# A hybrid decoder trunk on one core: block transposes and small tiles in a triangular inverse, and another order of entries, FFN ends, head and tail

## The reference

```python
for l in range(DEPTH):                                   # DEPTH = 2, D_FF = 2816
    h = rms_norm(x, ffn1_norm[l]); x = x + 0.5 * swiglu(h, w_gate, w_up, w_down)
    proj = rms_norm(x, mix_norm[l]) @ w_in[l]            # 1024 -> 3080
    aq, ak, av, pu, dq, dk, dv, dz, db, da = split(proj) # 3x256, 256, 4x512, 4, 4
    ya = dilated_attention(rope(aq), rope(ak), av)       # 4 heads of 64, 3 patterns
    yb = multiscale_pool(pu, pool_w[l], pool_scale[l])   # windows 2, 4, 8, 16
    yc = gated_deltanet(dq, dk, dv, dz, db, da, ...)     # 4 heads of 128, chunks of 64
    x = x + concat(ya, yb, yc) @ w_out[l]
    h = rms_norm(x, ffn2_norm[l]); x = x + 0.5 * swiglu(h, w_gate2, w_up2, w_down2)
return rms_norm(x, final_norm)
# in gated_deltanet, per head and chunk of 64 tokens (decay: a lower triangle):
A = strict_lower((k * beta) @ k.T) * decay
T = triangular_solve(eye + A, eye)                       # the inverse
u, w = T @ (v * beta), T @ (k * beta * exp(g))
```

## Time and profile before

| | before |
|---|---|
| median of 3 runs | 1093.78 us |
| profiled execution | 1093.62 us |
| its span in the trace | 1091.8 us |
| mean granted clock of PE | 0.997 of full speed |
| busy: PE, PE weight load, DVE, ACT, POOL | 97%, 84%, 67%, 56%, 21% |

### The profile page before, as it was taken

The page is one execution under the profiler, slowest core; times in us unless marked ns, Lnnn a source line. Parts: engine busy times, 40 slices in busy tenths (PEclk is TensorE's granted clock), DMA queues, the critical chain, the costliest instruction groups (busy, mean ns, idle before and its releaser), DMA issues.

```text
span 1091.8 us, 18536 instructions
## 1 busy us (share of the span) xinstructions
PE 1060.0 (97%) x6251; PEld 922.2 (84%) x6251; DVE 736.9 (67%) x1153; ACT 616.0 (56%) x1077; POOL 231.7 (21%) x257
## 2 busy tenths in 40 slices
PE   7999999899999999999999999999999999999997
PEld 6888888798987788888878888888988878888885
DVE  5666666878745766666676666668785657666665
ACT  6555555847644655555665555566665546555554
POOL 2212111295300121121122121112003003211212
PEclk9999999999999999999999999999999999999998
DMA  9766666562312476666646666666532035766660
GB/s 296 238 194 190 191 183 181 139 194 78 135 40 72 141 216 188 192 191 190 183 133 208 194 191 190 183 185 167 162 115 79 2 116 163 207 189 193 190 193 38
DMA packets 251895, 178.23 MB, mean 163 GB/s; under 512 B 5875, under 2 KB 237576, under 8 KB 251720
## 3 DMA queue, kind: packets, MB, share of 16 engines
q1 hardware_dynamic: 250880, 175.66, 54.3%
q0 software_dynamic: 336, 1.71, 0.4%
q10 hardware_dynamic: 632, 0.23, 0.1%
HBM read 176.53 MB, written 1.05 MB: 163 GB/s over the span
## 4 chain that ended last, share of the span: by engine, by line
PE 83%; DVE 10%; ACT 5%; issue 1%; DMA 0%; ACTq 0%; DVEq 0%
PE bank L678 28%; PE bank L681 15%; PE bank L660 11%; PE bank L661 10%; PE bank L662 10%; DVE Wl L1647 4%; PE bank L1015 2%; ACT Wh L1219 1%; DVE X L1692 1%; PE bank L991 1%; DVE xr L1823 1%; PE bank L723 1%; ACT X L1277 1%; DVE VT L1834 1%; DVE early L1865 1%
## 5 line engine op out<-in xcount | busy, mean ns | idle before, releaser
L1647 DVE TENSOR_TENSOR Wl<-raw,Wh 128x1024 fp32r<-128x1024 f32 x330 | 424.6, 1296 | 102.3 <-ACT Wh L1219 102.2
L1219 ACT ACTIVATE Wh<-raw 128x1024 fp32r<-128x1024 f32 x330 | 337.1, 1053 | 78.2 <-PE bank L662 75.6
L678 PE MATMUL bank<-X,Wh 128*128 128x512 f32 x1344 | 334.7, 391 | 0.0
L678 PEld LDWEIGHTS bank<-X,Wh 128*128 128x128 f32 x1344 | 246.7, 188 | 47.6
L577 POOL TENSOR_TENSOR gact<-gact,pooled 128x256 f32<-128x256 f32 x88 | 79.2, 900 | 626.4 <-DVE gact L1743 462.2
L681 PEld LDWEIGHTS bank<-X,Wl 128*128 128x128 f32 x1344 | 183.0, 190 | 14.0 <-DVE Wl L1647 1.2
L681 PE MATMUL bank<-X,Wl 128*128 128x256 f32 x1344 | 187.8, 283 | 0.0
L660 PE MATMUL bank<-Wh,aH 128*128 128x512 f32 x352 | 139.0, 395 | 2.0 <-DVE aL L1764 1.6
L661 PE MATMUL bank<-Wl,aH 128*128 128x512 f32 x352 | 138.0, 392 | 0.0
L662 PE MATMUL bank<-Wh,aL 128*128 128x512 f32 x352 | 137.1, 389 | 0.0
L1316 ACT ACTIVATE dec<-bank 128x256 f32<-128x256 f32 x88 | 33.6, 382 | 123.2 <-PE bank L681 122.2
(11 more groups left out here) (244 smaller groups left out, 1302.0 us busy)
## 6 DMA issues: line engine op xcount, KB each, us to landing
raw<-in_ffn_w_gate SPq DMA_DIRECT2D x88, 512.0 KB, 4.0
raw<-in_ffn_w_up SPq DMA_DIRECT2D x88, 512.0 KB, 3.7
raw<-in_ffn_w_down SPq DMA_DIRECT2D x88, 512.0 KB, 4.4
raw<-in_w_in SPq DMA_DIRECT2D x50, 512.0 KB, 3.9
raw<-in_w_out SPq DMA_DIRECT2D x16, 512.0 KB, 4.0
cst<-in_consts POOLq DMA_DIRECT2D x1, 1536.0 KB, 7.0
xr<-in_x SPq DMA_DIRECT2D x2, 512.0 KB, 4.4
norm_w<-in_final_norm SPq DMA_DIRECT2D x1, 512.0 KB, 5.7
```

The lines of the kernel that those rows point to most:

```text
L678: nc.tensor.matmul(b[:, :], piece(Wh, s)[:, k, :], X[:, k, :, :], start=k == 0, stop=False)
L1219: return nc.scalar.activation(Wh[:, s, :], raw[:, s, :], ACT.Copy).then_inc(hi_cast.sem, 1)
L1647: return nc.vector.tensor_tensor(Wl[:, s, :], raw[:, s, :], Wh[:, s, :].bitcast(F32), ALU.subtract).then_inc(lo_cast.sem, 1)
```

## The change

1. **Inverse.** LEVELS is (2, 4, 8, 16). There P is made of the even blocks' columns alone (64 of 128). The transposes on PE (8 for the start, 8 per level) and ACT's copies of them are gone: DVE makes DT from D, and the first D from dt0, by transposes of 32x32 blocks (128x512 in one instruction). Level 32 is `quarter_p` and `quarter_d` with tiles of 32x32, level 64 is `half_p` and `half_d` with tiles of 64x64. The casts of output pieces 29 and 30 leave the levels: Wh goes behind the last copies of the inverse, Wl behind `out_norm(1)`.
2. **Entry of the mixer.** `att_part` 6 and 7 move into the inverse (`att_late`, behind `quarter_p` and `half_p`) and use the scaled x. `row_root` stands behind j = 2. On DVE the splits 4 to 7 and the Wl of pieces 2 and 3 stand before the roots, the xs operations are cut in two around a Wl, and small copies (prm) come later. The entry of FFN2 and the next layer's FFN1 have the splits 4 to 7 earlier too, and FFN2's first two Wl among the updates of xr.
3. **End of an FFN.** `hid`, aH and aL of the last tile are made in two halves of 128 tokens; PE waits for each, and for aL only before the third product.
4. **Head and tail.** The norm weights' transfers move from ACT's queue to POOL's. In the tail DVE makes quarter (0,0) in one operation and scales (1,1), ACT scales (0,1) and (1,0), POOL weighs the last three quarters; four stores, three from SP and one from ACT.

```diff
-POS_GATES, POS_QK, POS_V, POS_Z, FIRST_OUT = 8, 9, 17, 21, 25
+POS_GATES, POS_QK, POS_V, POS_Z, POS_LATE, FIRST_OUT = 6, 7, 15, 19, 23, 25
-LEVELS = (2, 4, 8, 16, 32, 64)
+LEVELS = (2, 4, 8, 16)
...
+            for n, weight in enumerate((ffn1_norm, mix_norm, ffn2_norm)):
+                pool.dma_start(nrm_rows[n * DEPTH * KT:(n + 1) * DEPTH * KT, :],
+                              weight.rearrange("l (k c) -> (l k) c", c=P)).then_inc(norms_in.sem, 16)
...
+                    high, low_part, i = (half_ah, half_al, f + 1) if c == 0 else (ah_done, al_done, (f + 1) * TILES)
+                    pe.wait_ge(*high.at(layer, i))
+                    nc.tensor.matmul(acc[c][n][:, :], aH[:, 1, t], Wh[:, 5, q], start=False, stop=False)
+                    nc.tensor.matmul(acc[c][n][:, :], aH[:, 1, t], Wl[:, 5, q], start=False, stop=False)
+                    pe.wait_ge(*low_part.at(layer, i))
+                    return nc.tensor.matmul(acc[c][n][:, :], aL[:, 1, t], Wh[:, 5, q], start=False, stop=True)
...
+                            m = nc.tensor.matmul(bank[4 + c][odd, h * 32:(h + 1) * 32], LT[even, u, odd], Dm[even, u, even],
+                                                 start=True, stop=True)
...
+                        nc.tensor.matmul(bank[6 + c][q[1], at], DT[q[1], u, q[1]], PM[q[1], u, 0:32], start=True, stop=True)
+                        nc.tensor.matmul(bank[6 + c][q[0], at], PM[q[1], u, 0:32], DT[q[1], u, q[1]], start=True, stop=True)
+                        m = nc.tensor.matmul(bank[6 + c][q[2], at], PM[q[3], u, 0:32], DT[q[3], u, q[3]],
+                                             start=True, stop=True)
...
                 for n in range(len(LEVELS)):
                     for c in range(HALVES):
                         level_p(n, c)
-                    if n:
-                        for c in range(HALVES):
-                            turn_d(n - 1, c)
-                    if n == len(LEVELS) - 1:
-                        turn_qk()
                     for c in range(HALVES):
                         level_d(n, c)
+                for c in range(HALVES):
+                    quarter_p(c)
+                att_late(6)
+                for c in range(HALVES):
+                    quarter_d(c)
+                turn_qk()
+                for c in range(HALVES):
+                    half_p(c)
+                att_late(7)
+                for c in range(HALVES):
+                    half_d(c)
...
                 follow(3)
-                hidden_high(layer, f, TILES - 1, 1)
+                act.wait_ge(*half_mul.at(layer, f + 1))
+                act.wait_ge(*downs_done.at(layer, (f + 1) * TILES - 2))
+                nc.scalar.activation(aH[:, 1, 0:P], hid[:, 1, 0:P], ACT.Copy).then_inc(half_ah.sem, 1)
+                act.wait_ge(*mul_done.at(layer, (f + 1) * TILES))
+                nc.scalar.activation(aH[:, 1, P:], hid[:, 1, P:], ACT.Copy).then_inc(ah_done.sem, 1)
...
+                def turn_blocks(n, c):
+                    u = slice(4 * c, 4 * c + 4)
+                    dve.wait_ge(*d_done.at(layer, 2 * (n - 1) + c + 1))
+                    nc.vector.transpose(DT[:, u, :].rearrange("p u d -> p (u d)"),
+                                        Dm[:, u, :].rearrange("p u d -> p (u d)")).then_inc(dt_done.sem, 1)
...
                 out_norm(1)
+                lo_mix(layer, 29)
+                lo_mix(layer, 30)
                 dve.wait_ge(*att_hi.at(layer, 1))
```

More of the change, by code:

```diff
@@ L512, in weigh_final @@
                 pool.wait_ge(norm_w_in.sem, 16)
-                for i in range(3):
+                for i in range(1, 4):
                     c, b = divmod(i, 2)
@@ new lines, in half_p, with half_d @@
+                def half_p(c):
+                    pe.wait_ge(*d_done.at(layer, 8 + c + 1))
+                    for h, u in units(c):
+                        m = nc.tensor.matmul(bank[4 + c][EVEN:, h * EVEN:(h + 1) * EVEN], LT[0:EVEN, u, EVEN:],
+                                             Dm[0:EVEN, u, 0:EVEN], start=True, stop=True)
+                    m.then_inc(p_done.sem, 1)
+                def half_d(c):
+                    pe.wait_ge(*pm_done.at(layer, 10 + c + 1))
+                    pe.wait_ge(*dt_edge.at(layer, c + 1))
+                    for h, u in units(c):
+                        m = nc.tensor.matmul(bank[6 + c][0:EVEN, h * EVEN:(h + 1) * EVEN], PM[EVEN:, u, 0:EVEN],
+                                             DT[EVEN:, u, EVEN:], start=True, stop=True)
@@ L1298, in enter @@
                     square(1, 1)
-                    for c in range(HALVES):
-                        inverse(layer, n, c)
                 act.wait_ge(*turned.at(layer, 4 * n + 4))
@@ L1303, in enter @@
                     split(j)
-                if first:
-                    for c in range(HALVES):
-                        inverse(layer, n, c)
+                for c in range(HALVES):
+                    inverse(layer, n, c)
                 act.preload_act_table_set(SILU)
@@ L1505, in mixer @@
                 for c in range(HALVES):
-                    act.wait_ge(*d0_turned.at(layer, c + 1))
-                    nc.scalar.activation(Dm[:, 4 * c:4 * c + 4, :].rearrange("p u d -> p (u d)"), bank[4 + c][:, :],
-                                         ACT.Copy).then_inc(d_done.sem, 1)
-                for c in range(HALVES):
                     act.wait_ge(*v_turned.at(layer, c + 1))
@@ L1965, in new_values @@
+                for c in range(HALVES):
+                    dve.wait_ge(*p_done.at(layer, 10 + c + 1))
+                    nc.vector.tensor_scalar(PM[EVEN:, 4 * c:4 * c + 4, 0:EVEN],
+                                            bank[4 + c][EVEN:, 0:256].rearrange("p (u t) -> p u t", u=4), -1.0, None,
+                                            ALU.mult).then_inc(pm_done.sem, 1)
                 def new_values(c):
```

347 lines of the change are left out of this document (211 added, 136 removed).

## The result

The change made the kernel **slower** by 1.1%: 1105.68 us (median of 4 runs, 1105.02 to 1106.13) against 1093.61, the median of 4 runs of the kernel before; the ratio is 1.0108 with a 95% interval of 1.0096 to 1.0121. The forecast was 1079 with a range of 1071 to 1087.5.

The account below looks back on a forecast made before the run. PE, busy 97% of the span, was taken to bound the kernel with its few idle places. Two layers at 6.7 us gained, less 0.1, plus 0.4 and 1.0, made 14.7: 1079 us, range 1071 to 1087.5.

Parts of the forecast that it names:

- the walk of the inverse: Inverse, DVE's order followed: first D at 288.9, first product with V at 316.0 against 316.45; 0.1 us gained per layer.
- case 4: Inverse: small tiles empty the array, 0.2 us per 32x32 pass in place of 0.045; 1104 us, slower, chance 0.06.
- Halving the columns of P saves nothing on PE: Inverse levels: D with 64 columns and P with 128 cost the same, 0.115 and 0.118 us per pass.
- The entry: Entry of the mixer: 5.65 us of moved matmuls plus 0.7 less idle time, less 0.05; 6.3 us gained per layer.
- The level's period: Inverse: 3.6 us from one level's D to the next, through P, PM, D, copy and four hand-overs.
- The transpose: Inverse: DVE's block transpose of 128x512 takes 0.7 us, bounds 0.5 and 1.4.
- case 3: Inverse: DVE's transpose at 1.2 us, or longer hand-overs; 7.1 us gained in all, 1086.7 us, chance 0.16.
- Small tiles: Inverse levels 32 and 64: 112 passes at 0.045 us each, 5.0 us per layer, bounds 3.4 and 14.6.
- Output projection: Output projection: two Wl ahead of the att_lo subtraction put it at 339.2, a loss of 0.5 us per layer.
- FFN2 entry: FFN2 entry: x_new of the last quarter no longer waits for two Wl; 0.8 us gained per layer.
- Head: Kernel start: norm weights' transfers on POOL's queue end PE's first transpose wait; 0.4 us gained, 0 to 0.8.
- Tail: Kernel end: four stores, DVE and ACT sharing quarters, and half-size last FFN operations; 1.0 us gained, 0.2 to 1.6.

Follow-up runs that it names:

- f1_inverse: The kernel before with only the change's inverse; attention pieces 6 and 7 stay at the entry: 1111.85 us.
- e2_rope_late: The changed kernel with POOL's rotary products held until DVE has made the Wl of pieces 25 to 27: 1099.32 us.
- e3_casts_spread: The changed kernel with the Wl of pieces 25 to 28 made one behind each level's PM, instead of three ahead of the first: 1069.38 us.
- h4_best_wide: h1_best with P of levels 2 to 16 made of all 128 columns: 1066.68 us.
- h1_best: g1_head_lo with FFN ends in one piece except the very last, and the tail of the kernel before: 1066.80 us.
- f2_order: The change without its inverse, attention pieces 6 and 7 inside the last two old levels: 1089.79 us.
- g1_head_lo: e3_casts_spread with norm weights on ACT's queue again and the Wl of pieces 29 and 30 behind the first att_lo: 1067.89 us.
- g2_ffn_end: g1_head_lo with the last FFN tile's hid, aH and aL in one piece again, as before the change: 1067.76 us.
- e1_warm: The changed kernel with 16 extra thrown-away matmuls of 512 columns on PE between P and the inverse's first D: 1101.24 us.
- e4_before_gap: The kernel before with three extra DVE subtractions ahead of the Wl of piece 25, delaying the inverse's first D: 1110.59 us.
- h2_wide_p: The changed kernel with P of levels 2 to 16 made of all 128 columns, DVE reading only the even ones: 1084.75 us.
- h3_inverse_spread: f1_inverse with the Wl of pieces 25 to 28 made one behind each level's PM: 1075.97 us.

## Why the prediction was wrong, step by step

**The step that failed** is the walk of the inverse: "Now P of level 2 starts at 286.62, its D at 288.56, with DVE on its three Wl (283.55, 3.49 us) all the while" and, from there, every price at full clock. Two things in it were wrong. First, the Wl were not what the D waited for. Before, the Wl are through at 287.04, and PM is late because it waits for P:

```profile
287.81 0.69 DVE L1959 TENSOR_TENSOR PM<-bank,cst 128x512 f32<-128x512 f32 x1 [0.78 <-PE bank L991]
```

In the change it is the other way round. P comes earlier against DVE's work, by the 8 transposes that are gone from PE (0.87), and the Wl later, by a transpose of 0.7 behind each dt0, so P ends before the Wl do. (The 48 matmuls that moved have no part in this: f1_inverse leaves them ahead and has 3.75 us of idle time too.) The walk had the D behind the Wl, at 288.9, but never subtracted the end of P from it. By its own numbers P then starts near 285.75 and ends near 287.5, which is 1.4 us of idle time; e2_rope_late, where the Wl take 3.45, has 1.69. In the change they also lie beside POOL's products, take 5.60, and it is 3.84. Second, an idle time of that size was not paid once. It was followed by 27 us at 1.2 GHz, 12.9 us a layer (first D to first product 36.39 against 23.50 in e3_casts_spread).

**The sum without the clock** is the change less 2 x 12.9, 1079.9, where I had 1079. That the two numbers meet is in part luck. Counted from the end of FFN1, the walk has the first D at 91.5 us (288.9 less 6.3 and less 191.05), and it came at 93.95, 2.4 too late, of which 2.1 are the slower Wl. Against that it has 27.1 us from the first D to the first product (288.9 to 316.0), and at full clock it is 23.50: from the D of level 2 to that of level 4 it takes 5.6 where 3.57 were measured (281.25 to 284.82), and the stretch behind the levels is some 1.4 too long. With the idle time gone as well, e3_casts_spread takes 1069.4, below the range.

None of the five cases had the clock in it. The earlier trace rows show PE idle 0.66 and 0.56 us ahead of two D's at full clock; that a longer idle time might change the price of everything behind it was a case of its own, on the slower side, and it was missing. The chance of 0.06 for "slower" belonged to case 4, which did not come true.

**"Halving the columns of P saves nothing on PE. It only shortens what DVE does behind it."** True at 2.4 GHz (h4_best_wide against h1_best, 1066.7 and 1066.8). Once the clock was down they went with how long it stayed so: first D to first product took 36.39 us with 64 columns and 27.12 with 128.

**The entry**: 6.3 us and 0.87 for the transposes were forecast, 7.36 measured. Right, and f2_order shows it without the inverse. In the rows of the changed kernel that answer to the earlier trace rows, the wait of 0.40 for the last aL is gone, pieces 2 and 4 wait less, and the turn of x at the end of FFN1 (198.43) waits 1.00 us, where before it did not wait:

```profile
198.43 1.09 PE L698 MATMUL bank<-cst,xr 128*128 128x128 f32 x8 [1.00 <-DVE xr L1931]
...
208.30 0.39 PE L671 MATMUL bank<-Wh,X 128*128 128x256 f32 x1 [0.47 <-DVE Wl L1731]
...
215.19 0.39 PE L671 MATMUL bank<-Wh,X 128*128 128x256 f32 x1 [0.50 <-DVE Wl L1731]
...
346.48 0.47 PE L671 MATMUL bank<-Wh,X 128*128 128x512 f32 x1 [0.58 <-DVE X L2194]
...
363.92 1.09 PE L698 MATMUL bank<-cst,xr 128*128 128x128 f32 x8
```

**The level's period**: 3.6 us walked, 3.58 measured in e3_casts_spread (284.82 to 288.40). **The transpose**: 0.7 taken, 0.71 measured (279.01). The estimate from the Trainium skill's figure for 128x128 in two-byte elements ("VectorE: DVE Perf Modes", The three transpose paths), 1.24 us, is too high for four of them in float32: the measurement decides, and case 3 was none. **Small tiles**: I took 0.045 a pass. At full clock the 32 passes of the 32x32 P start within 0.79 us (0.025 each; e3_casts_spread, 293.85), the 48 of D within 0.51 (0.011; the change, 316.41 to 316.92), those of 64x64 at 0.061. With 32 passes of 64x64 that is 3.3 us a layer in place of 5.0. Case 4, at 0.2 a pass, was wrong by a factor of eight and more: in the 32x32 D each pass is in another tile than the one before it, and starts 0.01 us behind it while that one still runs (0.19 us), as "TensorEngine Tiling (Array Packing)" of the Trainium skill has it under Tiling Modes (tiles operate independently). The trace agrees.

**Output projection**: a loss of 0.5 forecast, 0.9 measured, of which 0.58 is the wait for att_lo (346.48 above) and g1_head_lo wins 0.8 back. **FFN2 entry**: 0.8 forecast, 1.1 measured; the turn at 363.92 no longer waits. **Head**: +0.4 forecast, no gain there. With the norms on POOL's queue PE's turn of them started between 7.69 and 8.91 in six executions, on ACT's between 7.55 and 7.92 in eight; the change's own profiled execution is the one with 8.91. **Tail**: 1.0 forecast, 0.2 measured (14.15 to 13.98 from the last gate or up matmul to the span's end). The halves of the last FFN give 0.7 (14.7 in g2_ffn_end, 14.0 in g1_head_lo) and the new tail takes 0.5 (14.0 against 13.5 in h1_best): POOL's three quarters still take 3.75 us, and DVE's one-column operations are slow beside them (0.73 us at 1095.62, against 0.22 at 1098.98 when POOL is through).

```profile
1093.81 3.75 POOL L525 TENSOR_TENSOR big<-xr,norm_w 128x512 f32<-128x512 f32 x3 [4.13 <-DVE xr L1931]
...
1095.62 0.73 DVE L1750 SCALAR_TENSOR_TENSOR stat<-stat 128x1 f32<-128x1 f32 x1
...
1100.37 0.38 ACTq L1344 DMA_DIRECT2D out_x<-big  x1
```

**What stays open.** Shown is that waits of 1.69 us and more between P and D were each followed by a fall (the change, e1_warm, e2_rope_late, e4_before_gap, f1_inverse, h2_wide_p), that without them the change's levels ran at full clock (e3_casts_spread), and that with the wait left in, 128 columns of P in place of 64 had the clock back after 7 us and not 27 (h2_wide_p). What the chip goes by is not shown: layer 1 of h3_inverse_spread fell without such a wait, and no run here was made to tell.

## What to carry to other kernels

After an edit that takes work off the busiest engine, subtract where its next wait now ends from where its work now ends, at every place that the edit moves, and let no new idle time stand on TensorE ahead of a stretch of short matmuls: here it was paid in the clock of the 27 us behind it. Work of another engine that isn't urgent (here four casts) belongs behind what TensorE waits for, one piece per step of the chain. Look at the granted clock by windows before looking for any other reason.
